# The up projection of block two as seven half-size products per weight slot, with its weight sums on GpSimd

## The reference

```python
D_FF_2, CONV_W = 2816, 3
def causal_dwconv(u, w, bias):
    S = u.shape[1]
    up = jnp.pad(u, ((0, 0), (CONV_W - 1, 0), (0, 0)))
    out = bias
    for j in range(CONV_W):
        out = out + w[j] * up[:, j:j + S]
    return out

# end of hybrid_layer; x is (1, 256, 1024), w_up (1024, 5632), w_down (2816, 1024)
    x = x + y @ w_out
    a, val = jnp.split(rmsnorm_2(x, norm_ffn_g) @ w_up, 2, axis=-1)
    a = causal_dwconv(a, conv_w, conv_b)
    return x + (jax.nn.gelu(a) * val) @ w_down
# the caller: return rmsnorm_2(x, norm_final_g)
```

## Time and profile before

| | |
|---|---|
| Runs before | 1728.39, 1731.82, 1732.13 us; median 1731.82 |
| The profiled execution | 1728.98 us, its span 1727.1 us, mean granted TensorE clock 0.995 |
| TensorE busy | 1654.0 us, 96% of the span |
| VectorE, ScalarE, GpSimd busy | 531.3, 245.9, 7.6 us |
| Up projection (L2253) | 154.7 us, begins at 1500.17 us of the span |
| Down projection (L2262) | 66.1 us, ends at 1720.9 us |

### The profile page before, as it was taken

How to read it: one execution, slowest core, us unless ns; L and a number is a source line. 1 busy time by engine, 2 the same in 40 slices (tenths; PEclk the granted TensorE clock), 3 DMA queues, 4 the chain that set the end, 5 groups by cost and what they waited for, 6 DMA issues and landing times.

```text
span 1727.1 us, 19612 instructions
## 1 busy us (share of the span) xinstructions
PE 1654.0 (96%) x7696; PEld 833.5 (48%) x7697; DVE 531.3 (31%) x1152; ACT 245.9 (14%) x508; POOL 7.6 (0%) x5
## 2 busy tenths in 40 slices
PE   5999999999999999999999999999999999999998
PEld 4767785433333333333333333232364787588853
DVE  2744432312212121212221212121231623144581
ACT  3014422101000000000000000000131321100010
POOL 0010000000000000000000000000000000000000
PEclk9999999999999999999999999999999999999999
DMA  9886227589999999999799999999974241434320
GB/s 404 338 280 257 98 110 256 222 364 430 428 428 428 428 429 428 428 429 429 283 429 429 428 429 428 428 429 427 430 304 146 98 147 66 190 146 147 146 73 25
DMA packets 46825, 528.70 MB, mean 306 GB/s; under 512 B 12752, under 2 KB 13152, under 8 KB 14784
## 3 DMA queue, kind: packets, MB, share of 16 engines
q1 hardware_dynamic: 36576, 521.16, 72.9%
q10 hardware_dynamic: 10208, 6.97, 1.4%
HBM read 527.05 MB, written 1.06 MB: 306 GB/s over the span
## 4 chain that ended last, share of the span: by engine, by line
PE 70%; DMA 25%; DVE 3%; issue 1%; ACT 1%; SPq 0%; DVEq 0%
DMA ring<-experts_dram 24%; PE scores L1997 17%; PE proj L1702 10%; PE proj L2253 9%; PE att_out L2034 7%; PE proj L1692 6%; PE proj L2262 4%; PE proj L1819 3%; PE proj L1857 3%; PE turned L1966 2%; DMA ring<-stream_dram 2%; PE scores L1896 1%; PE scores L1784 1%; PE att_out L1808 1%; PE proj L1744 1%
## 5 line engine op out<-in xcount | busy, mean ns | idle before, releaser
L1997 PE MATMUL scores<-ring,arena 128*64 128x512 f32 x2112 | 471.3, 594 | 21.5 <-DMA ring<-experts_dram 19.4
L1997 PEld LDWEIGHTS scores<-ring,arena 128*64 128x64 f32 x2112 | 149.3, 137 | 331.2 <-issue 275.1
L2034 PE MATMUL att_out<-ring,arena 128*64 128x512 f32 x1024 | 233.9, 598 | 0.0
L1702 PE MATMUL proj<-ring,arena 128*128 128x512 f32 x384 | 167.6, 594 | 2.5 <-DVE arena L1178 2.5
L1374 DVE COPY arena<-turned 128x512 f32<-128x512 f32 x33 | 22.8, 691 | 475.8 <-PE turned L1966 475.8
L2253 PE MATMUL proj<-arena,ring 128*128 128x256 f32 x704 | 154.7, 383 | 0.7 <-ACT arena L855 0.7
L2253 PEld LDWEIGHTS proj<-arena,ring 128*128 128x128 f32 x704 | 135.4, 193 | 19.9 <-ACT arena L855 1.1
L2034 PEld LDWEIGHTS att_out<-ring,arena 128*64 128x64 f32 x1024 | 68.0, 136 | 140.9 <-issue 140.9
L1702 PEld LDWEIGHTS proj<-ring,arena 128*128 128x128 f32 x384 | 72.1, 190 | 89.7 <-issue 86.4
L1692 PE MATMUL proj<-arena,ring 128*128 128x256 f32 x512 | 113.1, 381 | 0.0
L1692 PEld LDWEIGHTS proj<-arena,ring 128*128 128x128 f32 x512 | 96.5, 190 | 14.9 <-issue 1.8
(11 more groups left out here) (369 smaller groups left out, 1188.4 us busy)
## 6 DMA issues: line engine op xcount, KB each, us to landing
ring<-experts_dram SPq DMA_DIRECT2D x190, 2048.0 KB, 21.9
ring<-stream_dram SPq DMA_DIRECT2D x54, 2048.0 KB, 9.3
arena<-experts_dram SPq DMA_DIRECT2D x2, 2048.0 KB, 9.8
ring<-stream_dram SPq DMA_DIRECT2D x2, 1024.0 KB, 16.7
arena<-rpb_dram ACTq DMA_DIRECT2D x16, 128.0 KB, 3.4
arena<-gain_rows_dram ACTq DMA_DIRECT2D x3, 512.0 KB, 9.4
xtok<-xtok_dram SPq DMA_DIRECT2D x1, 1024.0 KB, 5.3
arena<-ctxtok_dram SPq DMA_DIRECT2D x1, 1024.0 KB, 7.5
```

Source lines behind the costliest of these rows:

```text
L1702: ins = mm(pb[:, 0:n], src[:, k, tt * P:tt * P + P], W[:, k, 0:n], start=k == 0, stop=k == KD - 1)
L1997: ins = mm(AS[n][parts, :], xe[:, k % 4, k // 4, :], W[:, kk, n * D + feats.start:n * D + feats.stop], start=False, stop=k == KD - 1, skip ...
L2034: ins = mm(AO[parts, :], act_s[:, kk, s - 4, :], W[:, kk, feats], start=s == 4 and kk == 0, stop=s == 5 and kk == 3)
```

## The change

The up projection of a slot is computed as a two by two block product with seven multiplications (Winograd's form). The halves are: the contraction (feature tiles 0 to 3 and 4 to 7), the tokens (tile 0, tile 1) and the column group j. Each of the seven products is 8 matrix products of 128 x 128 weights by 128 tokens into half a bank (`up_product`), so 56 a slot in place of 32, of half the columns. Order on TensorE: products 1 and 2 (they want only tile 0 of the tokens and untouched weights), then 5, 7, 6, 3, 4; 6 adds to the bank of 1, 3 to that of 5, 4 to that of 7. Products 1 and 2 of slots 0 and 1 stand ahead of the last two turns of tile 1 and of the remaining ten products of these slots. Slots take the four `PB` banks and the other four in turn; the down projection uses the latter.

- GpSimd: four operations of 1024 elements a partition for each slot. `early_up_sums(n)` (two of them) waits for the slot's landing and for product 5 of slot n - 2; `late_up_sums(n)` (two, which overwrite weights) waits for product 1 and for product 2 of the slot.
- VectorE: four operations of 128 x 512 once for the sums of tokens, and for each slot five additions of 128 x 256 that put the products together, four of them reading a bank; the convolution now reads `up_raw` in the arena; L1585 is folded into the multiplication (new L1734).
- ScalarE: three copies of 128 x 256 from a bank for each slot.
- The ring slot is freed by product 4 (`up_done`).
- The end: `gain_final` is loaded after the last up product; VectorE multiplies each half by the gain ahead of the inverse (one half of each tile while the down projection still runs), then one VectorE operation and one of ScalarE scale the two halves; the late half is stored first.

```diff
+            def early_up_sums(n):
+                pool.wait_ge(landed2[(UP0 + n) % RING], land2(UP0 + n))
+                if n >= 2:
+                    pool.wait_ge(up_done, up_at(5, n - 2))
+                nc.gpsimd.tensor_tensor(up_s1[n % 2], up_block(n, 0, 1), up_block(n, 1, 1), ALU.add)
+                nc.gpsimd.tensor_tensor(up_block(n, 0, 1), up_block(n, 0, 0), up_block(n, 0, 1), ALU.subtract)\
+                  .then_inc(up_sums, 1)
+
+            def late_up_sums(n):
+                pool.wait_ge(up_sums, n + 1)
+                pool.wait_ge(up_done, up_at(1, n))
+                nc.gpsimd.tensor_tensor(up_block(n, 0, 0), up_s1[n % 2], up_block(n, 0, 0), ALU.subtract)\
+                  .then_inc(up_sum2, 1)
...
+            early_up_sums(0)
+            early_up_sums(1)
+            for n in range(11):
+                late_up_sums(n)
+                if n + 2 < 11:
+                    early_up_sums(n + 2)
...
+            for s in range(11):
...
+                nc.scalar.activation(raw[:, :, 0, 0:P], up_half(X), ACT.Copy).then_inc(up_x_copied, 1)
+                if s:
+                    gelu_parts(s - 1)
+                act.wait_ge(up_done, up_at(5, s))
+                nc.scalar.activation(raw[:, :, 1, P:T], up_half(Z_), ACT.Copy).then_inc(up_z_copied, 1)
+                act.wait_ge(up_done, up_at(6, s))
+                nc.scalar.activation(up_u[s % 2], up_half(X), ACT.Copy).then_inc(up_u_copied, 1)
...
+            add_second(0)
             for s in range(11):
...
+                add_to_first_half(s)
+                convolve(s, 0)
+                add_to_second_half(s)
+                convolve(s, 1).then_inc(ffn_gate, 1)
+                dve.wait_ge(ffn_gate, 2 * s + 1)
+                step(V.scalar_tensor_tensor(out=raw[:, 1], in0=raw[:, 1], scalar=0.5, in1=cv, op0=ALU.mult,
+                                            op1=ALU.mult))
...
-            turn_normed(hn2, 2, 4)
-            turn_normed(hn2, 3, 4)
-            pe.wait_ge(hT_ready, 8)
-            for n in range(11):
...
+            def up_product(bank_, weights, tokens_, start=True):
+
+                for c in range(2):
+                    for k in range(4):
+                        ins = mm(bank_[:, c * P:c * P + P], weights[:, k, c, :], tokens_[:, k, :], start=start and c + k == 0,
+                                 stop=k == 3, skip_group_check=True)
+                ins.then_inc(up_done, 1)
...
+            pe.wait_ge(hT_ready, 6)
+            pe.wait_ge(x_half, 10)
+            up_from_first_tile(0)
             turn_normed(hn2, 2, 4)
             turn_normed(hn2, 3, 4)
+            up_from_first_tile(1)
+            pe.wait_ge(x_half, 12)
             pe.wait_ge(hT_ready, 8)
...
+            up_from_sums(0)
+            up_from_sums(1)
+            for n in range(2, 11):
+                up_from_first_tile(n)
+                up_from_sums(n)
...
             for tt in range(TT):
-                add_product(6 + tt, PB[2 + tt], tt, 1 - tt, done=True)
+                add_product(6 + tt, down_banks[2 + tt], tt, 1 - tt, done=True)
+                dve.wait_ge(x_half, 15 + tt)
+                times_gain(tt, 1 - tt)
                 token_mean(10 + tt)
-                token_rstd(10 + tt)
-                for h in range(2):
-                    V.scalar_tensor_tensor(out=final[:, tt, half_of(h)], in0=xtok[:, tt, half_of(h)],
-                                           scalar=tok_r[:, 10 + tt:11 + tt], in1=gain_final[:, half_of(h)],
-                                           op0=ALU.mult, op1=ALU.mult).then_inc(final_ready, 1)
+                inverse_root(10 + tt).then_inc(final_inv, 1)
+                dve.wait_ge(final_inv, tt + 1)
+                late = final[:, tt, half_of(LATE[tt])]
+                V.tensor_scalar(late, late, tok_r[:, 10 + tt:11 + tt], None, ALU.mult).then_inc(final_ready, 1)
```

More of the change, by code:

```diff
@@ L479, in two_blocks @@
         down_slots = sem("down_slots_used")
+        up_done = sem("up_product_done")
+        up_sums = sem("up_weight_sums_ready")
+        up_sum2 = sem("up_second_weight_sum_ready")
+        up_sum4 = sem("up_fourth_weight_sum_ready")
+        h_sums = sem("normed_token_sums_ready")
+        up_x_copied = sem("up_first_product_copied")
+        up_z_copied = sem("up_fifth_product_copied")
+        up_u_copied = sem("up_first_and_sixth_copied")
+        up_y_added = sem("up_second_product_added")
+        up_w_added = sem("up_seventh_product_added")
+        up_z_used = sem("up_third_product_used")
+        up_w_used = sem("up_fourth_product_used")
         ffn_act = sem("ffn_act")
@@ L482, in two_blocks, with up_at @@
         actT_ready = sem("actT_ready")
-        final_ready = sem("final_ready")
+        final_ready = sem("late_half_of_tile_scaled")
+        final_early = sem("early_half_of_tile_scaled")
+        gained = sem("early_half_times_gain")
+        final_inv = sem("final_token_factor_ready")
+        up_order = [(p, n) for n in range(2) for p in (1, 2)] + [(p, n) for n in range(2) for p in (5, 7, 6, 3, 4)]
+        up_order += [(p, n) for n in range(2, 11) for p in (1, 2, 5, 7, 6, 3, 4)]
+        def up_at(p, n):
+            return up_order.index((p, n)) + 1
         stream1 = [A["stream1"][n] for n in range(N_STREAM1)]
@@ L514, in two_blocks @@
         used2 += [(bank_done2, M2 + 8)] * 2 + [(bank_done2, M2 + 11), (bank_done2, M2 + 12)]
-        used2 += [(bank_done2, M2 + 12 + 2 * n + 2) for n in range(11)]
+        used2 += [(up_done, up_at(4, n)) for n in range(11)]
         used2 += [None] * 6
-        assert len(used2) == N2 and M2 + 12 + 22 == len(BANKS2)
+        assert len(used2) == N2 and M2 + 12 == len(BANKS2)
         G2 = 12 + 2 + 4
@@ new lines, in add_to_first_half @@
+            def add_to_first_half(s):
+                raw, u = up_raw[s % 2], up_u[s % 2]
+                _, _, Z_, W_ = up_banks[s % 2]
+                dve.wait_ge(up_z_copied, s + 1)
+                dve.wait_ge(up_done, up_at(7, s))
+                V.tensor_tensor(raw[:, :, 1, P:T], raw[:, :, 1, P:T], up_half(W_), ALU.add).then_inc(up_w_added, 1)
+                dve.wait_ge(up_w_added, s + 1)
+                dve.wait_ge(up_u_copied, s + 1)
+                V.tensor_tensor(raw[:, :, 1, P:T], raw[:, :, 1, P:T], u, ALU.add)
+                dve.wait_ge(up_done, up_at(3, s))
+                V.tensor_tensor(raw[:, :, 0, P:T], u, up_half(Z_), ALU.add).then_inc(up_z_used, 1)
+                dve.wait_ge(up_z_used, s + 1)
+                dve.wait_ge(up_y_added, s + 1)
@@ new lines, in up_from_sums @@
+            def up_from_sums(n):
+                X, _, Z_, W_ = up_banks[n % 2]
+                pe.wait_ge(up_sums, n + 1)
+                pe.wait_ge(h_sums, 1)
+                if n >= 2:
+                    pe.wait_ge(up_z_used, n - 1)
+                up_product(Z_, up_s1[n % 2], h_t1)
+                if n >= 2:
+                    pe.wait_ge(up_w_used, n - 1)
+                up_product(W_, up_block(n, 0, 1), h_block(0, 1))
+                pe.wait_ge(up_x_copied, n + 1)
+                pe.wait_ge(up_sum2, n + 1)
+                pe.wait_ge(h_sums, 2)
+                up_product(X, up_block(n, 0, 0), h_t2, start=False)
+                pe.wait_ge(up_z_copied, n + 1)
+                pe.wait_ge(up_sum4, n + 1)
+                up_product(Z_, up_block(n, 1, 0), h_block(1, 1), start=False)
+                pe.wait_ge(up_w_added, n + 1)
+                up_product(W_, up_block(n, 1, 1), h_t4, start=False)
```

166 lines of the change are left out of this document (109 added, 57 removed).

## The result

The changed kernel takes **1752.36 us** (median of 4 runs, 1750.90 to 1752.58), beside 1730.11 us of the kernel before on the same chip (4 runs, 1727.64 to 1732.13): ratio 1.0129, 95% interval 1.0115 to 1.0142. It is 22 us slower. Forecast were 1724 us and a range of 1706 to 1745: the sign was wrong, and the time is outside the range. The nearest of the rivals, "GpSimd always goes first", had 1743 us.

What follows compares the result with a forecast made beforehand. TensorE alone was taken to bound the up and down projections. With GpSimd and VectorE taking turns, the up projection's -3.9 and the end's -0.7 made 1728.98 - 4.6 = 1724.4, taken as 1724 us; range 1706 to 1745.

Steps and rivals of the forecast that it cites:

- GpSimd always goes first: Rival, up projection: each GpSimd sum stops VectorE's whole chain, 16.5 us a slot; 1743 us (1733 to 1750); chance 0.27.
- What bounded the kernel before: Up and down projection: TensorE alone, 154.66 and 66.11 us, so a matmul less is time saved if nobody is late.
- TensorE's stream: Up projection: 1232 matmuls of 128 columns at 0.113 us, 139.2 us in place of 152.0, so -12.8 us.
- The start: Up projection's first products cover the norm of tile 1: gap shrinks by 4.6 us, slow clock stretch goes, -2.6 us.
- The end: Behind the last down product: VectorE 0.43 us beside ScalarE 0.6 us where 1.42 us stood, so -0.7 us.
- the price of the collision: Up projection: GpSimd's 7.4 and VectorE's 6.5 us add to 13.9 us a slot; stage ends 3.9 us earlier.
- I take turns op by op with no loss at the handover: Likeliest case, up projection: GpSimd's and VectorE's on-chip memory operations alternate, together 155.0 us; 1715 to 1732 us, chance 0.38.
- the length of a sum: GpSimd, up projection: 1.86 us for 1024 elements, from 4096 in 7.44 us; 7.4 us for a slot's four.
- VectorE's bank reads give GpSimd 1.7 us a slot for nothing: Up projection: argument against GpSimd going first, that GpSimd runs unhindered during VectorE's bank reads, 1.7 us a slot.
- The rule on the lock: Skill's rule: VectorE with two on-chip inputs and GpSimd share a port pair as an exclusive lock; result then on slower side.
- The seven products don't pay: Rival, up projection: at 0.125 us per 128-column matmul a slot costs the same as now; "little chance", start still gives 7 us.
- The chances: Taking turns 0.38, no collision (1708 us) 0.32, GpSimd first 0.27, anything else 0.03.

Runs made afterwards that it cites:

- e11: Changed kernel without GpSimd's weight sums and with the early start undone (both turns of tile 1 ahead of all products): 1716.64 us, ratio 0.9926.
- e12: Repeat of e1, the changed kernel without weight sums, on the same chip as e11: 1710.20 us, ratio 0.9882.
- e3: Changed kernel with each GpSimd weight sum cut into four operations of 256 elements: 1725.26 us, ratio 0.9970.
- e9: Changed kernel with the two early sums of each slot whole on GpSimd, the two late ones on VectorE: 1731.77 us, ratio 1.0009.
- e5: Kernel before, plus three GpSimd operations (additions, one-input multiplications or fills) in each of nine slots, into memory nothing else uses: 1727.55 us, one run.
- e10: Changed kernel with each GpSimd weight sum replaced by a one-input multiplication by 0.5 of the same 1024 elements: 1711.27 us, ratio 0.9892.
- e1: Changed kernel without GpSimd's 44 weight sums and TensorE's waits for them: 1708.07 us, ratio 0.9878.
- e2: Changed kernel with all 44 weight sums on VectorE, placed where it waits for others: 1710.90 us, ratio 0.9894.
- e6: e2 with the early start undone (both turns of tile 1 ahead of all products): 1723.25 us, ratio 0.9957.

## Why the prediction was wrong, point by point

**What bounded the kernel before** was read rightly, and so was what TensorE gains. Without the sums the stage is 21.7 us shorter (1654.67 less 1631.94, less 1.00 from ahead of it); forecast were 20.0.

**TensorE's stream: -14.4 in place of -12.8** (the 21.7 less the 7.3 of the start). A steady slot takes 12.5 us and a matmul (3.74 - 0.275)/31 = 0.112 us, between my ends of 0.108 and 0.116 and a little under the 0.113 that I took.

**The start: -7.3 by e11 and e12**, as forecast (-4.6 and -2.6). In the changed kernel most of it is lost: from the stage's first product to product 2 of slot 1 it takes 11.7 us (1494.23 to 1505.92), in e12 6.2. I had counted no work of VectorE in the first six products. But the norm of tile 1 falls there, and the two late sums of slot 0, which start at 1496.33 us, fall on it: its two halves take 5.35 us in place of 1.42 (e12).

```profile
1496.33 2.35 POOL L678 TENSOR_TENSOR ring<-arena,ring 128x1024 f32<-128x1024 f32 x1 [49.00 <-PE proj L2396]
1496.63 5.35 DVE L1501 SCALAR_TENSOR_TENSOR arena<-xtok,small,arena 128x512 f32<-128x512 f32 x2
```

**The end: about -0.3 in place of -0.7.** From the last addition (1744.61 us) to the end of the span are 5.9 us, before 6.1. ScalarE's half took 0.72 us, not 0.6, and the stores followed as before. The down projection kept its 66.1 us.

**The step that failed is the price of the collision**, where I wrote: "I take turns op by op with no loss at the handover". It made 13.9 us a slot out of GpSimd's 7.4 and VectorE's 6.5. Between 1569.63 and 1633.30 us four rounds took 63.67 us, 15.9 each. Three things were wrong in it.

First, the length of a sum. I took a quarter of the earlier trace rows, 1.86 us. A sum takes 2.35 where VectorE is not in its way (the changed kernel, ahead of the stage), 9.4 us a slot:

```profile
1442.49 2.35 POOL L671 TENSOR_TENSOR arena<-ring 128x1024 f32<-128x1024 f32 x1 [13.82 <-DMA ring<-stream_dram]
```

With it my own way of adding gives 9.4 + 6.5 = 15.9 us a slot, and by the same steps 1743 us for the kernel (an estimate: 94.0 + 80.6 in place of 155.0, with 7.1 lost at the start in place of 8.1). This one price turned the sign of the forecast.

Second, the way of adding is no rule, though it meets the steady rounds here. It has one of the two engines always working and never both. With the sums in quarters it would give more than with whole ones, since a sum in four pieces takes 2.96 us with VectorE hardly in its way (e3):

```profile
1445.52 2.96 POOL L672 TENSOR_TENSOR arena<-ring 128x256 f32<-128x256 f32 x4 [12.89 <-DMA ring<-stream_dram]
```

Four of these and 6.5 are 18.3 us, and a slot took 13.7. For e9 it gives 13.5 (two sums of 2.35, 6.5, and two of 1.14 on VectorE), and a round took 14.3 (1574.91 to 1589.18 us). The rival's way, VectorE's whole chain of 8.2 + 0.9 plus four stops, is on the other side: with the stops of the timeline, 7.6, it gives 16.7 for the changed kernel. So the 15.9 of both the corrected sum and the trace is in part luck. What the rows do show is why a stop is dear: VectorE's operations hang on each other, on two ScalarE operations and on bank reads, and in the time that remains GpSimd stands still (5.3 to 6.3 us in each of these rounds), since its sums wait for products of the same slot.

Third, I argued against the rival that "VectorE's bank reads give GpSimd 1.7 us a slot for nothing"; a bank read does pass unhindered (L1691), but only this one of the four meets a sum.

**The rival "GpSimd always goes first" had the mechanism and the place**: the waits are for L1069 behind the gelu and for L1700. Its 16.5 us a slot was 0.6 over the steady rounds, out of two errors that nearly cancel: sums 2.0 us a slot too short, and every one of them counted in full against VectorE. It missed what lies around the steady rounds: the start, 5.5 us longer than in e12; a wait of TensorE of 6.3 us at 1522 to 1528 for the tanh of slot 0, behind three stretched operations, so that slots 0 and 1 did not run at 12.7; one slot with first sums of down weights that took 18.0; and the clock at 0.50 for some microseconds behind five of the waits. Between 1500 and 1680 us TensorE stood still for 30.9 us by its windows. These lie between 1743 and 1752; how much each of them gives was not measured apart. My range ended at 1745, which left out the upper part of the rival's own 1733 to 1750 and would not have held 1752 even with it.

**The rule on the lock.** The trace of before could not decide; the changed kernel's, e5's and e10's do. By the Trainium skill (SBUF — State Buffer, Who interferes with whom) a VectorE instruction with two on-chip inputs contends with a GpSimd instruction that reads on-chip memory, not with one that only writes it, and the one with one such input and no fast mode contends with none. By this rule the forecast would have been on the slower side, and the rows agree: L1738 is held, L1691 isn't, and beside the probe's fills the two-input operation kept its 0.69 us. The same page of the Trainium skill has it that the lock is held for the whole instruction. For the sums the trace agrees (L1734 waits out the 2.36 us of L678); for the one-input operation the runs measure otherwise (L1734 loses 0.83 us beside one of 2.93, and L1738, begun 2.1 us into it, nothing), and the measurement decides.

**"The seven products don't pay"** is refuted by e1. **The chances**: faster 0.55 and 0.27 for the rival that came. What should have moved them was at hand: VectorE's chain is serial and had 3.6 us of room in a slot (9.1 of 12.7), less than four stops of even 1.86 us, and the middle between two ends was a choice for lack of a row.

## What to carry to other kernels

Before a helper engine gets work, measure whether its operations hold off those of the engine that it is to help: the same operation's length beside them and without them shows it. Take the price of the helper's operation from one of the same form, not from a part of a larger one (1.86 against 2.35 us). If they hold each other off, ask whether the other engine's serial chain has room for the stops, and forecast with both ways of adding: the work of both engines, and the chain plus its stops. The rounds with whole sums lay at the first (15.9 of 15.9 and 16.7) or between the two (14.3 of 13.5 and the 15.4 that e9's expectation had at worst). Where an engine has room, give it the work itself: VectorE at 96% busy cost some 3 us, GpSimd at 59% cost 44. If the helper must be used, try its operations in pieces: of four sizes here quarters were the best.

## What was not expected of the hardware

A GpSimd multiplication with one input (2.77 to 3.0 us for 1024 elements) is slower than an addition of two (2.1), yet shuts VectorE out for only about its first microsecond (0.83 us of 2.93 in e10). Cutting a sum of 2.35 us into four makes GpSimd's part longer (3.0 to 3.8 us) and the kernel 27 us faster; into eight, 31 us slower again. What sets the 4 to 5 us by which traces of nearly the same kernel come to the stage sooner or later (1491.78 us in e12, 1496.59 in e2, for the same four products) was not looked into and stays open. That e2's trace is one of its late ones is the likely reason why the medians of e2 and e6 are further apart than their traces.
